# Two-layer trunk in split fp32r on one core: another warm-up for TensorE ahead of the first product

## The chip, the cores and the metric

The kernel runs on one core of a Trainium2 chip. The metric is the device time of one execution in microseconds (us). Three executions of the kernel before are shown; their median is 2297.53 us.

## The reference, cut to what matters

One sequence of 256 tokens of width 2048 passes through two layers. Layer 0 mixes tokens with a gated MLP (a causal 128 x 128 matrix for each of 16 groups of channels), layer 1 with dilated attention (24 heads of 128, three dilations). Behind each stands a gated FFN with a causal convolution of width 3. The matrix products are nearly all of the work:

```
h = x
h = h + gmlp(rms_norm(h))          # w_in 2048 x 4096, w_s 16 x 128 x 128, w_out 2048 x 2048
h = h + conv_ffn(rms_norm(h))      # w_gate, w_up 2048 x 5632, w_down 5632 x 2048
h = h + dilated_attention(rms_norm(h))   # w_qkv 2048 x 9216, w_o 1024 x 2048
h = h + conv_ffn(rms_norm(h))
return rms_norm(h)
```

Everything is float32.

## The kernel before

Activations lie transposed, with channels on the 128 partitions and the 256 tokens along the row. Each float32 operand is split in two fp32r parts, a high one (a rounded copy) and a low one (the rest). `X[:, kt, :]` holds 512 columns: 256 of the high part, then 256 of the low part.

All weights come as one stream of 784 units of 512 KB. A unit is eight tiles of 128 x 128 side by side. SP loads unit after unit into a ring of four slots (`raw`); ACT rounds a unit into `w_hi` (line 439), DVE subtracts and writes `w_lo` (line 728), and PE then works through the eight tiles in `multiply` (lines 1017 to 1028). Two matmuls belong to each tile: line 1026 multiplies `w_hi` with all 512 columns, line 1027 multiplies `w_lo` with the 256 high columns and adds into the same bank. ACT may write a slot of `w_hi` only when PE has finished the unit before in that slot (`units_done`), and SP loads a slot again when `w_lo` has been made from it (`lo_ready`).

The order is fixed by the program text of each engine; there is no planner. PE goes through V and U of the gated MLP (256 pairs of matmuls each), its output product (256), gate and up of the first FFN (1408), down (704), eight heads of attention (144 each), the output product (128), and the second FFN (1408 + 704), 6272 pairs in all. Into this stream the small matmuls of the norms (`mean_square`, plain float32, lines 1048 to 1053), the token mixing, the transposes and the attention scores are set at written places. Long stretches are loops (`Fori`).

At the start ACT issues five loads of `x`, makes the high part of `X` (line 565), and squares `h` for the first norm, with the splits of units 2 to 5 set between the squares. DVE zeroes `hidden`, `warm_r` and `warm_b`, then makes the low part of `X` (`x_low`, line 744) and the `w_lo` of the units. POOL clears small tiles, adds the squares up, and then loads `WS` and `BS`. The tiles `warm_r` and `warm_b` lie where `GX` is written much later. PE waits for both to be zeroed and runs its warm-up (lines 1080 to 1082) into bank `acc[1][:, 1]`, which the first product needs only in its second pair of output blocks and then starts afresh: 16 matmuls of 512 columns and 8 of 128 in fp32r, and 6 of 512 in bf16. Then it waits for `cleared` and `ident_set`, and starts the V product, whose every tile waits for its block of `X` (`x_ready`).

Of the kernel before, what the change touches and what calls it, by code (L numbers as in the profile page):

```python
# [31 lines left out]
F32R = mybir.dt.float32r  # L32
BF16 = mybir.dt.bfloat16
# [4 lines left out]
P = 128  # L38
S = 256
D = 2048  # L40
KT = D // P
# [87 lines left out]
def trunk(nc, w_stream, x_t, vecs_d, ws_t, bs_row, mask_d, rope_d, out):  # L129
    with ExitStack() as ctx:  # L130
# [3 lines left out]
        def sem(name):  # L134
            return ctx.enter_context(nc.semaphore(name))
# [35 lines left out]
        def place(name, at, shape, dt=F32):  # L171
            assert at + int(np.prod(shape[1:])) * 4 <= arena_bytes
            return nc.alloc_sbuf_tensor_at(name, shape, dt, offset=arena_at + at)
# [3 lines left out]
        BLK = S * 4  # L177
# [3 lines left out]
        at = 4 * KT * BLK  # L181
# [5 lines left out]
        vsum = place("vsum", at + 4 * BLK, [P, 2, S])  # L187
        ln_rinv = place("ln_rinv", at + 6 * BLK, [P, S])

        warm_r = place("warm_r", 2 * KT * BLK, [P, 2 * S], F32R)  # L190
        warm_b = place("warm_b", 2 * KT * BLK + 2 * BLK, [P, 2 * S], BF16)

        OX = place("OX", 0, [P, HEADS, 2 * S], F32R)
        at = HEADS * 2 * BLK
# [20 lines left out]
        acc = [ctx.enter_context(nc.psum_tensor(f"acc{i}", [P, 2, 2 * S], F32)) for i in range(2)]  # L215
# [29 lines left out]
        warm_set = sem("warm_set")  # L245
# [185 lines left out]
        def _(act):  # L431
# [218 lines left out]
            def softmax_exp(h_):  # L650
                for t, (a, b, _) in enumerate(score_parts):
                    act.wait_ge(maxed, 2 * h_ + t + 1)
                    nc.scalar.activation(sm[:, a:b], sm[:, a:b], ACT.Exp, bias=nmax[:, t:t + 1],
                                         accum_out=rsum[:, t:t + 1]).then_inc(exped, 1)
# [66 lines left out]
        def _(dve):  # L721
# [102 lines left out]

            nc.vector.memset(warm_r[:, :].bitcast(F32), 0.0).then_inc(warm_set, 1)
            nc.vector.memset(warm_b[:, :], 0.0).then_inc(warm_set, 1)

            dve.wait_ge(vecs_landed, 16)
            x_low(0, 0)
# [111 lines left out]
            def mask_scores(h_):  # L941

                dve.wait_ge(mask_landed, 16)
                dve.wait_ge(scored, h_ + 1)
                for a, b, c in score_parts:
                    nc.vector.scalar_tensor_tensor(sm[:, a:b], sc_flat[:, c:c + b - a], float(E) ** -0.5, mask[:, a:b],
                                                   ALU.mult, ALU.add).then_inc(masked, 1)
                for t, (a, b, _) in enumerate(score_parts):
                    dve.wait_ge(masked, 2 * h_ + t + 1)
                    nc.vector.reduce_max(nmax[:, t:t + 1], sm[:, a:b], AX_X, negate=True).then_inc(maxed, 1)  # L950

            def normalize(h_):

                dve.wait_ge(exped, 2 * h_ + 2)
                nc.vector.reciprocal(rrec[:, :], rsum[:, :]).then_inc(rsum_inv, 1)
                dve.wait_ge(rsum_inv, h_ + 1)
                for t, (a, b, _) in enumerate(score_parts):
                    nc.vector.tensor_scalar(sm[:, a:b], sm[:, a:b], rrec[:, t:t + 1], None, ALU.mult)\
                        .then_inc(normed, 1)
# [56 lines left out]
        def _(pe):  # L1016
# [60 lines left out]
                                    pe.wait_ge(hid_ready, FB * (layer + 1) + 1)  # L1077
                            multiply(ud + 44 * i + 11 * c + n, (11 * c + n) % RING, tiles_of(c % 2, hid, FB, n), needs)

            pe.wait_ge(warm_set, 2)  # L1080
            for n, (tile, cols) in enumerate(((warm_r, 512),) * 16 + ((warm_r, P),) * 8 + ((warm_b, 512),) * 6):
                nc.tensor.matmul(acc[1][:, 1, 0:cols], tile[:, 0:P], tile[:, 0:cols], start=True, stop=True)
            pe.wait_ge(cleared, 5)
            pe.wait_ge(ident_set, 1)
            product(U_V, P_V, KT // 2, X, KT, normed_ready(0), 0, ms_at=5)
# [257 lines left out]
```

## Time and profile before

| | before |
|---|---|
| three executions | 2297.53, 2315.18, 2285.84 us |
| the profiled execution: its span | 2297.4 us |
| its own time beside that span | the median of the runs shown is 2297.53 us |
| mean granted TensorE clock | 0.997 |
| PE busy | 2277.3 us (99%) |
| DVE, ACT, POOL busy | 1488.4, 1272.9, 104.4 us |
| 784 weight loads | 413 MB with the rest of queue q1, 54.0% of 16 DMA engines |

PE is TensorE's matmul stream, PEld its weight loads, which overlap it. Matmul ends are modelled, so one matmul's duration is longer than the distance to the next one's start; distances between starts are the safer measure. PEclk is the clock granted to TensorE, where 1.00 is 2.4 GHz and 0.50 is 1.2 GHz. In a window, a count in brackets takes in an instruction that began before the window and ended in it.

### The profile page before, as it was taken

The page shows a single profiled execution, that of the slowest core. Times are in us where ns is not written, and L with a number is a line of the kernel's source. Part 1 is how long each engine was busy: PE and PEld are TensorE (multiplying, and loading weights), DVE is VectorE, ACT ScalarE, POOL GpSimd, SP SyncE. Part 2 cuts the span into 40 slices and gives each one's busy share as a digit, 9 for nine tenths or more (in the row PEclk, how much of TensorE's full clock was granted, in tenths as well). Part 3 has the DMA queues.
Part 4 walks back from the last instruction along what each step waited for, and adds up shares of the span by engine and source line. Part 5 has one row for each costly group of instructions (what it writes and reads, how often), then busy time and mean ns, then how long its engine had stood idle before and what let it go on. Part 6 is the DMA issues. An engine that isn't in the chain of part 4 may idle for free.

```text
span 2297.4 us, 38095 instructions
## 1 busy us (share of the span) xinstructions
PE 2277.3 (99%) x13098; PEld 1990.5 (87%) x13098; DVE 1488.4 (65%) x1764; ACT 1272.9 (55%) x1587; POOL 104.4 (5%) x85
## 2 busy tenths in 40 slices
PE   8999999999999999999999999999999999999998
PEld 6888888888888888888888888888888888888887
DVE  6678666666666655556666666687677666665444
ACT  5455466666666644444555545556666666654443
POOL 3122100000000000000000000010000000000000
PEclk8999999999999999999999999999999999999999
DMA  6544555555555555555545545546555555556553
GB/s 242 192 161 163 189 184 183 183 188 186 185 188 184 184 190 184 185 178 209 166 166 170 167 165 172 169 153 195 189 191 184 191 191 191 187 189 192 188 188 136
DMA packets 115477, 419.21 MB, mean 182 GB/s; under 512 B 12832, under 2 KB 12960, under 8 KB 115168
## 3 DMA queue, kind: packets, MB, share of 16 engines
q1 hardware_dynamic: 114192, 413.43, 54.0%
q0 software_dynamic: 512, 2.95, 0.3%
q10 hardware_dynamic: 720, 2.10, 0.2%
q8 instruction: 37, 0.61, 0.1%
q14 instruction: 16, 0.13, 0.0%
HBM read 416.33 MB, written 2.10 MB: 182 GB/s over the span
## 4 chain that ended last, share of the span: by engine, by line
PE 96%; DVE 1%; POOL 1%; issue 1%; ACT 0%; DMA 0%; ACTq 0%; DVEq 0%; POOLq 0%
PE acc L1026 61%; PE acc L1027 31%; DVE X L744 1%; POOL vsum L402 1%; PE sc_ps L1164 0%; PE sc_ps L1144 0%; PE sc_ps L1151 0%; DMA h<-x_t 0%; PE acc L1207 0%; PE sc_ps L1159 0%; PE sc_ps L1143 0%; PE misc L1135 0%; DMA raw<-w_stream 0%; DVE w_lo L728 0%; ACT U L600 0%
## 5 line engine op out<-in xcount | busy, mean ns | idle before, releaser
L1026 PE MATMUL acc<-X,w_hi 128*128 128x512 f32 x4480 | 1582.8, 398 | 7.6 <-DVE X L744 6.4
L728 DVE TENSOR_TENSOR w_lo<-raw,w_hi 128x1024 fp32r<-128x1024 f32 x784 | 969.4, 1242 | 527.1 <-ACT w_hi L439 526.3
L1027 PE MATMUL acc<-X,w_lo 128*128 128x256 f32 x4480 | 1256.6, 281 | 0.0
L439 ACT ACTIVATE w_hi<-raw 128x1024 fp32r<-128x1024 f32 x784 | 825.4, 1058 | 469.7 <-PE acc L1027 462.7
L1026 PEld LDWEIGHTS acc<-X,w_hi 128*128 128x128 f32 x4480 | 842.1, 188 | 208.2 <-DVE X L744 5.6
L1027 PEld LDWEIGHTS acc<-X,w_lo 128*128 128x128 f32 x4480 | 848.5, 189 | 0.4
L1026 PE MATMUL acc<-hid,w_hi 128*128 128x512 f32 x1408 | 492.9, 395 | 0.0
L1027 PE MATMUL acc<-hid,w_lo 128*128 128x256 f32 x1408 | 394.9, 281 | 0.0
L1026 PEld LDWEIGHTS acc<-hid,w_hi 128*128 128x128 f32 x1408 | 264.0, 187 | 61.8
L1027 PEld LDWEIGHTS acc<-hid,w_lo 128*128 128x128 f32 x1408 | 266.4, 189 | 0.0
L449 ACT ACTIVATE hc<-acc 128x512 f32<-128x512 f32 x104 | 62.1, 597 | 160.0 <-PE acc L1027 160.0
L733 DVE TENSOR_TENSOR tsum<-hc,acc 128x512 f32<-128x512 f32 x104 | 71.5, 687 | 101.3 <-ACT hc L449 101.3
L367 POOL TENSOR_TENSOR ssum<-ssum,sq 128x512 f32<-128x512 f32 x24 | 33.1, 1378 | 1293.3 <-ACT sq L452 1293.3
L1026 PE MATMUL acc<-GX,w_hi 128*128 128x512 f32 x256 | 90.6, 399 | 1.0 <-DVE GX L863 1.0
L509 ACT ACTIVATE conv<-gu,vecs 128x256 f32<-128x256 f32 x88 | 53.0, 603 | 62.8 <-DVE gu L752 62.8
L752 DVE TENSOR_TENSOR gu<-tsum,rinv 128x512 f32<-128x512 f32 x104 | 72.4, 696 | 3.6
L1027 PE MATMUL acc<-GX,w_lo 128*128 128x256 f32 x256 | 71.9, 281 | 0.0
L632 ACT ACTIVATE hc<-acc 128x512 f32<-128x512 f32 (+1 forms) x40 | 22.2, 555 | 82.1 <-PE acc L1027 82.1
L459 ACT ACTIVATE X<-h,vecs x48 | 21.8, 502 | 73.8 <-DVE h L761 73.5
L1026 PEld LDWEIGHTS acc<-GX,w_hi 128*128 128x128 f32 x256 | 48.1, 188 | 13.1 <-DVE GX L863 1.3
L744 DVE SCALAR_TENSOR_TENSOR X<-h,vecs,X (+1 forms) x64 | 43.5, 707 | 23.1 <-ACT X L459 19.6
L439 ACT ACT_TABLE_LOAD x44 | 56.5, 1283 | 0.9
(141 smaller groups left out, 1080.2 us busy)
## 6 DMA issues: line engine op xcount, KB each, us to landing
raw<-w_stream SPq DMA_DIRECT2D x784, 512.0 KB, 3.4
out<-out_sb SPq DMA_DIRECT2D x8, 256.0 KB, 2.8
h<-x_t ACTq DMA_DIRECT2D x3, 512.0 KB, 6.9
WS<-ws_t POOLq DMA_DIRECT2D x1, 1024.0 KB, 8.1
BS<-bs_row POOLq DMA_DIRECT2D x1, 1024.0 KB, 11.1
mask<-mask_d POOLq DMA_DIRECT2D x1, 576.0 KB, 3.8
h<-x_t ACTq DMA_DIRECT2D x2, 256.0 KB, 4.7
rope<-rope_d POOLq DMA_DIRECT2D x1, 256.0 KB, 3.0
```

The costliest lines, as they stand in the source:

```text
L367: nc.gpsimd.tensor_tensor(ssum[:, :], ssum[:, :], sq[:, :, :].rearrange("p a b -> p (a b)"), ALU.add).then_inc(ss_added, 1)
L402: nc.gpsimd.tensor_tensor(vsum[:, :, :], vsum[:, :, :], U[:, 12 + 2 * k:14 + 2 * k, :], ALU.add)\
L439: nc.scalar.activation(w_hi[slot][:, :], raw[slot][:, :], ACT.Copy).then_inc(hi_ready, 1)
L449: nc.scalar.activation(hc[:, :, :], acc[s][:, :, 0:S], ACT.Copy).then_inc(hcopied, 1)
L509: nc.scalar.activation(conv[:, :], gu[:, 0, 2:S + 2], ACT.Identity, bias=vecs[:, one(cv + 3 * FB + j)], scale=vecs[:, one(cv + 2 * FB + j) ...
L632: nc.scalar.activation(hc[:, 0:n, :], acc[(par + m) % 2][:, 0:n, 0:S], ACT.Copy).then_inc(hcopied, 1)
L728: nc.vector.tensor_tensor(w_lo[slot][:, :], raw[slot][:, :], w_hi[slot][:, :], ALU.subtract)\
L733: nc.vector.tensor_tensor(tsum[:, :, :], hc[:, :, :], acc[s][:, :, S:2 * S], ALU.add)\
L744: nc.vector.scalar_tensor_tensor(X[:, 2 * pr + b, S:2 * S], h[:, 2 * pr + b, :], vecs[:, one(GAINS[n] + 2 * pr + b)], X[:, 2 * pr + b, 0:S ...
L752: nc.vector.tensor_tensor(gu[:, :, 2:S + 2], tsum[:, :, :], over(rinv, 2), ALU.mult)\
L1026: nc.tensor.matmul(bank, hi, moving[:, kt, :], start=first, stop=False)
L1027: op = nc.tensor.matmul(bank[:, S:2 * S], lo, moving[:, kt, 0:S], start=False, stop=last)
```

## The change

The warm-up is replaced by a longer one on larger zero tiles. `warm_r` grows from 512 to 4096 columns, a plain float32 tile `warm_n` of 512 columns is added, and PE waits for three memsets in place of two. The eight 128-column matmuls go. Behind the other 22 come: the pattern of a tile in `multiply` (512 columns, then 256 added into the upper half of the bank), eight times for each of eight shifts of the moving operand (0 to 128 columns) and eight times each for two passes that read it backwards; 16 matmuls of 512, 12 of 256 and 8 of 384 columns; four times two of 512 and two of 256; four of 512 and four of 256 in plain float32; and eight of 512 whose moving operand is two halves 512 columns apart. All write the same bank of `acc[1]`. Nothing that the output depends on is changed.

```
@@ trunk: tiles
-        warm_r = place("warm_r", 2 * KT * BLK, [P, 2 * S], F32R)
-        warm_b = place("warm_b", 2 * KT * BLK + 2 * BLK, [P, 2 * S], BF16)
+        warm_r = place("warm_r", 2 * KT * BLK, [P, 8 * 2 * S], F32R)
+        warm_n = place("warm_n", 2 * KT * BLK + 16 * BLK, [P, 2 * S])
+        warm_b = place("warm_b", 2 * KT * BLK + 18 * BLK, [P, 2 * S], BF16)
@@ vector
             nc.vector.memset(warm_b[:, :], 0.0).then_inc(warm_set, 1)
+            nc.vector.memset(warm_n[:, :], 0.0).then_inc(warm_set, 1)
@@ tensor
-            pe.wait_ge(warm_set, 2)
-            for n, (tile, cols) in enumerate(((warm_r, 512),) * 16 + ((warm_r, P),) * 8 + ((warm_b, 512),) * 6):
+            pe.wait_ge(warm_set, 3)
+            for n, (tile, cols) in enumerate(((warm_r, 512),) * 16 + ((warm_b, 512),) * 6):
                 nc.tensor.matmul(acc[1][:, 1, 0:cols], tile[:, 0:P], tile[:, 0:cols], start=True, stop=True)
+
+            bank = acc[1][:, 1, :]
+            M0 = 2048
+
+            def w_tile(n):
+                return warm_r[:, n % 8 * P:(n % 8 + 1) * P]
+
+            def pairs(shift, count=8, back=False):
+                for n in range(count):
+                    at = M0 + shift + n % 2 * 512
+                    first, second = warm_r[:, at:at + 512], warm_r[:, at:at + S]
+                    if back:
+                        first, second = warm_r[:, at + 511:at - 1:-1], warm_r[:, at + S - 1:at - 1:-1]
+                    nc.tensor.matmul(bank, w_tile(2 * n), first, start=True, stop=False)
+                    nc.tensor.matmul(bank[:, S:2 * S], w_tile(2 * n + 1), second, start=False, stop=True)
+
+            def single(cols, count, at=M0):
+                for n in range(count):
+                    nc.tensor.matmul(bank[:, 0:cols], w_tile(n), warm_r[:, at:at + cols], start=True, stop=True)
+
+            for shift in (0, 2, 4, 8, 16, 32, 64, 128):
+                pairs(shift)
+            pairs(0, back=True)
+            pairs(4, back=True)
+            single(512, 8)
+            single(512, 8, M0 + 4)
+            single(256, 12)
+            single(384, 8)
+            for n in range(4):
+                for k in range(2):
+                    nc.tensor.matmul(bank, w_tile(4 * n + k), warm_r[:, M0:M0 + 512], start=True, stop=True)
+                for k in range(2):
+                    nc.tensor.matmul(bank[:, 0:S], w_tile(4 * n + 2 + k), warm_r[:, M0:M0 + S], start=True, stop=True)
+            for cols in (512, 256):
+                for n in range(4):
+                    nc.tensor.matmul(bank[:, 0:cols], warm_n[:, n * P:(n + 1) * P], warm_n[:, 0:cols], start=True, stop=True)
+            for n in range(8):
+                view = warm_r[:, M0:M0 + 1024].rearrange("p (a b) -> p a b", b=512)[:, :, 0:S]
+                nc.tensor.matmul(bank, w_tile(n), view, start=True, stop=True)
```

## Rows read from the trace of the kernel before

**Rows 1.** The profile's page: header, busy time by engine and the chain of waits by engine.
```profile
span 2297.4 us, 38095 instructions
PE 2277.3 (99%) x13098; PEld 1990.5 (87%) x13098; DVE 1488.4 (65%) x1764; ACT 1272.9 (55%) x1587; POOL 104.4 (5%) x85
PE 96%; DVE 1%; POOL 1%; issue 1%; ACT 0%; DMA 0%; ACTq 0%; DVEq 0%; POOLq 0%
```

**Rows 2.** Timeline of DVE from 0: start us, us, engine line op out<-in xcount [idle before].
```profile
1.27 0.48 DVE L825 MEMSET warm_r<- 128x512 f32 x1
1.76 0.27 DVE L826 MEMSET warm_b<- 128x256 uint32 x1
5.41 0.88 DVE L744 SCALAR_TENSOR_TENSOR X<-h,vecs,X 128x256 fp32r<-128x256 f32 x2 [3.38 <-ACT X L565]
```

**Rows 3.** Timeline of PE, then a window: length, PE busy (count), PEclk.
```profile
2.08 6.10 PE L1082 MATMUL acc<-warm_r 128*128 128x512 f32 x24 [2.08 <-DVE warm_b L826]
8.03 1.47 PE L1082 MATMUL acc<-warm_b 128*128 128x512 bf16 x6
9.40 0.47 PE L1026 MATMUL acc<-X,w_hi 128*128 128x512 f32 x1
...
2.10:5.10 3.00, 3.00 (x7) 1.00 0.86 285
```

**Rows 4.** Windows of PE through the start.
```profile
20.00:26.00 6.00, 3.56 (x9) 0.50 0.00 0
28.00:30.00 2.00, 2.00 (x11) 0.80 0.56 201
```

**Rows 5.** Timeline of PE, then of DVE, 15 to 30 us.
```profile
15.92 0.76 PE L1026 MATMUL acc<-X,w_hi 128*128 128x512 f32 x1 [3.50 <-DVE X L744]
29.09 0.40 PE L1026 MATMUL acc<-X,w_hi 128*128 128x512 f32 x1
...
15.29 8.37 DVE L744 SCALAR_TENSOR_TENSOR X<-h,vecs,X 128x256 fp32r<-128x256 f32 x8
```

**Rows 6.** Timeline of PE around 34 us and the first mean square.
```profile
34.02 0.40 PE L1026 MATMUL acc<-X,w_hi 128*128 128x512 f32 x1
34.27 0.28 PE L1027 MATMUL acc<-X,w_lo 128*128 128x256 f32 x1
34.39 0.40 PE L1026 MATMUL acc<-X,w_hi 128*128 128x512 f32 x1
...
38.63 1.03 PE L1052 MATMUL misc<-ssum,mean_w 128*128 128x256 f32 x4
39.84 0.40 PE L1026 MATMUL acc<-X,w_hi 128*128 128x512 f32 x1
```

**Rows 7.** Windows of line 1026 alone: length, PE busy (count), PEld busy (count), PEclk.
```profile
29.09:38.62 9.53, 9.53 (x28) 4.96 (x27) 1.00 0.87 323
40.00:142.00 102.00, 101.37 (x293) 54.75 (x292) 1.00 0.57 191
320.00:1097.00 777.00, 776.38 (x2198) 412.77 (x2198) 1.00 0.56 186
1123.00:1153.00 30.00, 30.00 (x86) 15.96 (x85) 1.00 0.50 172
1515.00:1555.00 40.00, 40.00 (x114) 21.24 (x113) 1.00 0.56 184
1566.00:2285.00 719.00, 719.00 (x2076) 387.88 (x2075) 1.00 0.56 185
```

**Rows 8.** Timeline of ACT, DVE and POOL around 30 us.
```profile
30.41 1.06 ACT L439 ACTIVATE w_hi<-raw 128x1024 fp32r<-128x1024 f32 x1 [4.00 <-PE acc L1027]
...
34.32 1.23 DVE L728 TENSOR_TENSOR w_lo<-raw,w_hi 128x1024 fp32r<-128x1024 f32 x1 [1.59 <-ACT w_hi L439]
...
29.19 0.70 POOL L379 DMA_DIRECT2D WS<-ws_t  x1
```

**Rows 9.** Timeline of PE at 145 us.
```profile
145.16 1.13 PE L1100 MATMUL misc<-vsum,mean_w 128*128 128x256 f32 x4 [2.02 <-POOL vsum L402]
```

## The prediction, made before the result was known

> **What bounds the kernel now.** First the header, the engine totals and the chain of waits [rows 1]: the span is 2297.4 us, PE is busy for 99% of it, and 96% of the chain that ended last is PE. So time changes here in two ways only: PE is handed more or less work, or one piece of work takes PE longer. The profiled execution took the 2297.53 us that is also the median of the three runs shown (2285.84 to 2315.18), so the sum is made against 2297.5.
>
> Second, the start. The zero tiles are set by 2.03 us [rows 2], PE's old warm-up runs from 2.08 to 9.4 us and the first real product starts at 9.40 [rows 3]. But PE is not fed yet: it stands still for 3.50 us before 15.92, its granted clock falls from 1.00 to 0.50 (2.4 to 1.2 GHz), at half clock it is busy for 3.56 of 6.00 us between 20 and 26, and it is back at full clock within the window from 28 to 30 [rows 4, 5]. From 29.09 us on nothing holds it. The products (called pairs here: a 512-column matmul with `w_hi` and a 256-column one with `w_lo`) that started before 29.09 number 21 (eight of unit 0, eight of unit 1, five of unit 2). At the 0.35 us of a pair [rows 6] these are 7.4 us of work. So the start up to 29.09 is worth as much as a PE that begins fully fed at 29.09 - 7.4 = **21.7 us**. That is the number against which a longer warm-up is priced: up to there it costs nothing, since PE would be waiting anyway.
>
> Third, the long stretches at line 1026, where each row counts hi matmuls in a window [rows 7]. They show two rates at the same full clock and with PE busy throughout: 777 us for 2198 from 320 us on (353.7 ns a pair, the one that began before the window left off; first FFN), 719 us for 2076 from 1566 on (346.5 ns; second FFN). Both stages run the same code on operands of the same shapes. Short stretches are of one kind or the other: 9.53 us for 27 before the first mean square is slow (353), 102 us for 293 behind it quick, 40 us for 114 slow again (354). The rate does not drift; it changes where the stream of pairs is broken by a wait or by other matmuls, and then stays. I call this the **spacing**, and it is the only thing in this trace that could make the three runs differ by 29 us: one FFN layer has 2112 pairs, and 2112 x 6.6 to 7.2 ns is 14 to 15 us. The shown profile has one layer slow and one quick.
>
> **The change part by part.**
>
> *Memsets.* DVE sets `warm_r` with 4096 elements a partition in place of 512, and `warm_n` with 512. 512 took 0.48 us and the 256 words of `warm_b` took 0.27 [rows 2], so 0.82 ns for each further element: 0.48 + 3584 x 0.82 ns = 3.4 us, and 0.48 for `warm_n`. The DVE queue is then at 1.27 + 3.4 + 0.27 + 0.48 = 5.4 us. Behind them in that queue stands the first `x_low`, which started at 5.41 after 3.38 us of waiting for ACT: hidden, with no margin. PE waits for all three and starts at 5.45 rather than 2.08.
>
> *PE's new warm-up.* Removed: eight 128-column matmuls. Kept: 16 of 512 in fp32r, six in bf16. Added: 80 pairs (eight shifts and two reversed passes, eight each), 16 + 8 (mixed) + 8 (strided view) of 512, 12 + 8 of 256, 8 of 384, and in plain fp32 four of 512 and four of 256. Prices at full clock: a hi matmul takes its successor 0.23 us later and a lo one 0.12 us later, 0.35 together [rows 6]; 384 columns lie between, 0.175; the six bf16 took 1.37 us [rows 3]; the mean square, two plain fp32 matmuls of 256, put the next pair but one from 38.63 to 39.84, 1.21 us where a pair takes 0.35, so 0.43 us for 256 plain columns and 0.86 for 512 [rows 6].
> 80 x 0.35 = 28.0; 48 of 512 x 0.23 = 11.0; 20 of 256 x 0.12 = 2.4; 8 x 0.175 = 1.4; bf16 1.4; plain 4 x 0.86 + 4 x 0.43 = 5.2. Sum **49.4 us**.
> The first stretch runs at half clock: in the first 3.00 us of the old warm-up only seven fell, 0.43 us each [rows 3], twice the 0.23 of later rows. If the new one needs the same 3 us to be given the full clock, that is seven matmuls by 0.2: 1.4 us more. Warm-up ends at 5.45 + 49.4 + 1.4 = **56.2 us**.
>
> A rule bears on this term. The Trainium skill (TensorE: Matmul & The Clock Gate, Back-to-back issue gap) gives N / 2.4 + 2.5 ns for a warm matmul; as an estimate from that page the non-plain 97,280 columns would take 41.1 us where my rows give 44.2, and the end would be near 53 us. The rows for fp32r with its weight load each time decide here.
>
> *Unknown forms.* No row of the trace shows a shifted, reversed or strided fp32r read. Lower end: they cost as a plain one, since the array takes one column after another. Upper end: the nearest row for a slow read of four-byte data is plain fp32, 0.43 us per 256; a pair would be 1.3 us. For the 16 reversed pairs alone that is 16 x 0.95 = + 15 us; for the 56 shifted ones too, and the eight views at 0.86, + 74. I take the lower end: the row nearest in type and size is the fp32r pair itself. By the Trainium skill (SBUF — State Buffer, on the 16-byte lines) reads that hit a line at least twice run at full bandwidth; a reversed or shifted run of fp32 hits most lines four times, which also speaks for it.
>
> *What starts when PE is free.* Everything that held PE up to 28.8 us is done while it warms: `x_low` ends at 23.66 [rows 5], and the two `w_lo` splits behind it, 1.23 us each [rows 8], fill the last of the four slots before 27. Unit 4's slot comes free only when unit 0 is done. That is 8 x 0.35 = 2.8 us after the warm-up; ACT 1.06 and DVE 1.23 [rows 8] make it ready 5.1 us after, and it is wanted after 32 pairs, 11.2 us. In ACT's queue the squares of blocks 12 to 15 stand behind that split, so POOL's last two sums and its issue of the `WS` and `BS` loads behind them, at 29.19 before, slip to some 7 us after the warm-up (2.8, then 1.06 for the split, then the squares and sums); before they stood 29.2 - 21.7 = 7.5 us after the equivalent start [rows 8]. So they keep their place against PE, and the mean square, GELU sums and the 2.02 us wait at 145.16 [rows 9] move along unchanged. SP's queue gets its loads earlier than it needs. No stall is added and none but those of the start goes.
>
> *Sum.* 56.2 - 21.7 = + 34.5 us, so 2297.5 + 34.5 = **2332 us** (+ 1.5%), if each later stretch keeps the spacing it has.
>
> **The rivals.**
>
> 1. *Base case, 2332* (2322 to 2340 from the clock and the price of 128 to 512 columns). For it: the start is a clean sum. Whatever the warm-up does to the spacing is overwritten early: the first two windows [rows 7] show that the mean square at 38.63 alone changes it, and more breaks follow, as the wait at 145 [rows 9]. Chance 0.44.
>
> 2. *Slow side, over + 2%: the second FFN draws the slow spacing.* Place: the break at about 1558 us where the normed activations are waited for. Price: 2112 x 6.6 to 7.2 ns = 14 to 15 us, so 2332 + 14.5 = 2346. In the windows the stretch just ahead of that break is slow and the one behind it quick [rows 7], so the break is what set it. It decides as soon as that one layer is slow and the first one has not turned quick. The highest of the three runs, 17.7 us over the median, looks like this case. A like sum comes if the reversed pairs cost as plain fp32 does: 2347. Chance 0.26 together.
>
> 3. *The warm-up works: PE is left in the quick spacing and keeps it.* Then the slow stretches shown (2198 + 114 counted pairs, and 86 in each of eight heads [rows 7], together 3000) lose some 7 ns each: - 21 us, 2311. With the first FFN alone quick, 2317. The lowest run, 11.7 us under the median, looks like this half. Against it: breaks follow the warm-up and each of the heads repeats its own changes of spacing whatever came before. Still + 0.5% or more, since 34.5 is more than all there is to win. Chance 0.25.
>
> 4. *Faster than before.* It needs a spacing that no row shows: from 346 ns down to 320 (768 columns at 2.4 GHz) the 6272 pairs would lose 163 us, 2169. It decides from 6 ns a pair on average. Nothing in the trace speaks for it. Chance 0.03.
>
> 5. *The change does not do what it says*: the warm-up ends inside the 21.7 us in which PE has nothing to do, and the time stays at 2298. It would need less than half of the price of every row above. Chance 0.02.
>
> **How the numbers follow.** What a measurement of this kernel can tell is about 2%, 46 us: slower means above 2343.5. That is rival 2: 0.26. Faster, below 2251.6, is rival 4: 0.03. The rest, 0.71, is within. The predicted time is the base case. The range goes down to rival 3 with the short stretches that I left out (2310) and up to just past rival 2 (2349).
>
> **What would show it.** In the new profile: PE's first matmul at about 5.4 us; the first real product at 56 us (54 to 60); granted clock 1.00 from about 8 us on without a fall; no PE idle from there to the mean; the shifted and reversed groups with the mean of the unshifted ones; then two or three long windows whose length over count is either 346 to 348 or 352 to 354 ns. The span minus (old span + delay of the first real matmul against 21.7) must equal the pairs that changed spacing times 6.6 to 7.2 ns. I am wrong if the first real matmul comes after 65 us (forms cost), or if the spacing takes a new value.

## The result and the profile after

| | before | changed |
|---|---|---|
| executions | 2285.84, 2297.53, 2315.18 us | 2321.56, 2335.11, 2350.81 us |
| median | 2297.53 us | 2335.11 us |
| span of the profiled execution | 2297.4 us | 2319.8 us |
| PE busy | 2277.3 us (99%) | 2300.9 us (99%) |

The changed kernel takes 1.0146 times the time of before, 95% interval 1.0074 to 1.0218: slower, by 1.5% as measured, with 2% still inside the interval. The forecast was 2332 us in a range of 2310 to 2349; the median lies 3 us above the one and inside the other, the slowest execution 2 us outside. One execution of a later kernel, at a mean granted clock of 0.851 (2467.67 us, its other eleven at most 2301.32), is left out of every figure below. The profiled execution is the fastest of the three (2321.56 us), so its rows must be read beside one execution of the kernel before that was in the middle of its three.

The page after, header, engine totals and chain by engine, against [rows 1]:

```profile
span 2319.8 us, 38552 instructions
PE 2300.9 (99%) x13326; PEld 2018.3 (87%) x13326; DVE 1490.8 (64%) x1765; ACT 1270.0 (55%) x1587; POOL 103.9 (4%) x85
PE 97%; DVE 1%; POOL 1%; ACT 0%; issue 0%; DVEq 0%; ACTq 0%; POOLq 0%
```

PE still sets the end alone. Its queue starts later, behind three memsets. DVE's timeline after, against [rows 2]:

```profile
2.02 3.47 DVE L826 MEMSET warm_r<- 128x4096 f32 x1 [0.80 <-issue]
5.49 0.27 DVE L827 MEMSET warm_b<- 128x256 uint32 x1
5.82 0.48 DVE L828 MEMSET warm_n<- 128x512 f32 x1
6.22 0.75 DVE L745 SCALAR_TENSOR_TENSOR X<-h,vecs,X 128x256 fp32r<-128x256 f32 x2
```

The long memset took 3.47 us (3.4 forecast), but it began at 2.02 and not at 1.27. `x_low` slipped from 5.41 to 6.22. PE's timeline and two windows of line 1098 (the hi matmuls of the 80 pairs; length, PE busy with the count, PEld busy with the count, PEclk, DMA share, GB/s), against [rows 3]:

```profile
6.36 5.30 PE L1084 MATMUL acc<-warm_r 128*128 128x512 f32 x16 [6.36 <-DVE warm_n L828]
11.51 1.47 PE L1084 MATMUL acc<-warm_b 128*128 128x512 bf16 x6
```

```profile
12.62:35.00 22.38, 22.38 (x64) 12.01 (x64) 1.00 0.36 123
35.00:40.60 5.60, 5.60 (x17) 2.95 (x16) 1.00 0.00 0
```

```profile
57.24 0.40 PE L1028 MATMUL acc<-X,w_hi 128*128 128x512 f32 x1
```

The old part of the warm-up starts at 6.36. The window from 12.62 to 35.00 holds the eight shifts: 22.38 us for 64 pairs, 0.350 us each. The one from 35.00 to 40.60 holds the starts of the two reversed passes (16 hi matmuls; the seventeenth began before). It ends within a pair, so their price is better read from start to start:

```profile
34.93 0.40 PE L1098 MATMUL acc<-warm_r 128*128 128x512 f32 x1
...
40.94 0.62 PE L1103 MATMUL acc<-warm_r 128*128 128x512 f32 x2
```

From the last shifted pair to the first matmul behind the reversed ones lie 17 pairs in 6.01 us, 0.354 each. The groups of eight shifted pairs lie between 0.346 and 0.354. The first real product starts at 57.24. Windows of PE alone (length, busy with the count, PEclk), against [rows 4]:

```profile
6.40:9.40 3.00, 3.00 (x7) 1.00 1.02 419
14.00:57.00 43.00, 43.00 (x230) 1.00 0.16 58
57.00:80.00 23.00, 23.00 (x133) 1.00 0.49 187
1576.00:1578.50 2.50, 0.38 (x3) 1.00 0.56 184
1579.40:1582.80 3.40, 3.40 (x13) 0.51 0.64 219
```

In the first window the seven 512-column matmuls are 0.43 us apart, twice the 0.23 of later ones, as in [rows 3]: they ran at half clock although the column says 1.00. From 14 to 80 us PE is busy without a gap and the clock does not fall. It falls once, much later: PE had little to do from 1576.0 to 1578.5, and the 3.4 us behind 1579.4 ran at a granted clock of 0.51, close to the 1.2 GHz level. Last, line 1028 alone, which is line 1026 of before, against [rows 7]:

```profile
76.00:142.00 66.00, 66.00 (x191) 35.64 (x191) 1.00 0.56 193
258.00:353.00 95.00, 95.00 (x270) 50.51 (x270) 1.00 0.56 187
356.00:1117.00 761.00, 760.37 (x2194) 411.15 (x2193) 1.00 0.56 190
1588.00:2308.00 720.00, 720.00 (x2078) 388.37 (x2078) 1.00 0.55 185
```

Less the one that began before, 95 us for 269 is 353 ns a pair, 761 for 2193 is 347, 720 for 2077 is 346.7. In this execution **both** feed-forward layers have the quick spacing; in the one shown of before only the second had.

### The profile page after: what moved, and what is told of

It is laid out like the page before. It is cut to its first block, busy times and chain, and to the rows that moved or that the text cites. A ratio compares the mean times of both kernels' runs of the same rounds, so it can differ in the third digit from the quotient of the medians.

```text
span 2319.8 us, 38552 instructions
## 1 busy us (share of the span) xinstructions
PE 2300.9 (99%) x13326; PEld 2018.3 (87%) x13326; DVE 1490.8 (64%) x1765; ACT 1270.0 (55%) x1587; POOL 103.9 (4%) x85
## 4 chain that ended last, share of the span: by engine, by line
PE 97%; DVE 1%; POOL 1%; ACT 0%; issue 0%; DVEq 0%; ACTq 0%; POOLq 0%
PE acc L1028 61%; PE acc L1029 31%; PE acc L1098 1%; POOL vsum L403 1%; PE sc_ps L1205 0%; PE sc_ps L1185 0%; PE acc L1099 0%; PE sc_ps L1192 0%; PE acc L1084 0%; PE acc L1103 0%; PE acc L1248 0%; PE sc_ps L1200 0%; PE sc_ps L1184 0%; PE misc L1176 0%; PE acc L1120 0%
```

## The experiments

Twelve runs followed, one of them the changed kernel again. The kernel before ran beside them and, with its first three, has 97 executions. They fall on three levels with nothing between:

| level | range, us | mean | executions of before |
|---|---|---|---|
| low | 2281.67 to 2289.33 | 2285.0 | 41 |
| middle | 2297.53 to 2303.31 | 2300.5 | 35 |
| high | 2312.35 to 2317.30 | 2315.0 | 21 |

The steps are 15.5 and 14.5 us; the prediction had 14 to 15 us for one feed-forward layer at the other spacing. The traces bear that out. In all 14 of them a layer's loop runs at 346.7 or at 353.3 ns a pair from start to start. Nine executions with no slow layer are at the low level of their kernel, three with one (the first) at the middle one, and two with both at the high one. Theory 1 was: the delay is the warm-up's length past 21.7 us, and the level is drawn later, at breaks of PE's stream. Theory 2: the warm-up, or its forms, sets the spacing.

### No warm-up

```
-            for n, (tile, cols) in enumerate(((warm_r, 512),) * 16 + ((warm_r, P),) * 8 + ((warm_b, 512),) * 6):
-                nc.tensor.matmul(acc[1][:, 1, 0:cols], tile[:, 0:P], tile[:, 0:cols], start=True, stop=True)
```

> The kernel before without any warm-up matmul (the output is not touched by them). Theory 1 (time is the length of the warm-up past the start that the data allow, and spacing is redrawn at later waits whatever the warm-up was): PE begins the first eight pairs at half clock, which ends inside its own wait; the pairs from 29.09 us on stand as before, so the time is that of the kernel before within 2 us at the same spacing, on one of its three levels (2285, 2298, 2313). Theory 2 (the warm-up sets the spacing of the later stages): without it both feed-forward layers take one and the same spacing in every execution, most likely the slow one, 2311 to 2316 each time.

Ten executions: one at 2284.39, seven from 2299.97 to 2302.21, two at 2314.43 and 2314.78. Against before 1.0022 (0.9974 to 1.0071). Windows of PE, columns as above, and the longest wait of PE up to 40 us (total, times, longest):

```profile
9.20:13.40 4.20, 4.11 (x13) 1.00 0.96 344
16.00:24.00 8.00, 4.76 (x15) 0.75 0.21 72
24.00:29.00 5.00, 3.80 (x12) 0.50 0.28 105
29.00:33.00 4.00, 4.00 (x21) 0.84 0.81 248
```

```profile
PE acc L1026 <- DVE w_lo L728: 10.5, 2, 9.3
```

Full clock comes about 1.5 us later than before (within 29 to 33 at 0.84, where before the window from 28 to 30 had 0.80), and the first mean square starts at 39.07, where before it was 38.63 [rows 6]. So the old warm-up bought 0.4 us, next to nothing, as the reckoning with 21.7 us says, and all three levels appear without it.

The row from 9.2 to 13.4 reads 1.00, but the first pairs ran at half clock, as expected:

```profile
10.07 0.63 PE L1026 MATMUL acc<-X,w_hi 128*128 128x512 f32 x1
10.71 0.63 PE L1026 MATMUL acc<-X,w_hi 128*128 128x512 f32 x1
...
13.26 0.39 PE L1026 MATMUL acc<-X,w_hi 128*128 128x512 f32 x1
```

Their starts are 0.64 us apart up to 12.63 and 0.35 behind 13.26. Ahead of the first change of clock in a trace the distances must be read, not the column PEclk. Theory 2 falls in its plain form.

### As long, of one form

```
-            for shift in (0, 2, 4, 8, 16, 32, 64, 128):
-                pairs(shift)
...
-                nc.tensor.matmul(bank, w_tile(n), view, start=True, stop=True)
+            pairs(0, 127)
```

> The changed kernel with its many forms replaced by as long a stretch of one form: 22 old matmuls, then 127 unshifted pairs. Theory 1: the forms are nothing, the length all; first real product at 57 us (56.5 to 58), time on the same three levels as the changed kernel (2321, 2335, 2350), and breaks later redraw the spacing. Theory 2: the later spacing goes by the forms, so all executions come out alike and off those of the changed kernel, at the slow level, 2350.

```profile
57.67 0.40 PE L1028 MATMUL acc<-X,w_hi 128*128 128x512 f32 x1
```

First real product at 57.67 us; four executions at 2320.75, 2321.89, 2333.28 and 2335.65; 1.014 of before (1.0039 to 1.024). The same delay and the low and middle levels of the changed kernel. The unshifted pairs are 0.353 us apart here, start to start, so the reversed ones above (0.354) cost no more. The forms can be exchanged without a trace in the time; four executions are too few to say anything of the shares.

### Cut to what the start hides

```
-        warm_r = place("warm_r", 2 * KT * BLK, [P, 8 * 2 * S], F32R)
+        warm_r = place("warm_r", 2 * KT * BLK, [P, 4 * 2 * S], F32R)
...
+            pairs(0)
+            pairs(4)
+            pairs(0, back=True)
```

(in place of all groups behind the first 22 matmuls, with `M0 = 512`)

> The changed warm-up cut to what the start hides: 22 old matmuls, then 8 unshifted, 8 shifted by 4 and 8 reversed pairs, on a warm_r of 2048 columns. It should end near 20 us. Theory 1: the granted clock does not fall in the first 30 us, the pairs of unit 1 and 2 run at 0.35 instead of 0.64, and the first product that nothing holds comes at most 1 us sooner against its count; time on the levels of the kernel before, less 0 to 1 us. The rival to the sum: the warm-up costs its own length wherever it ends, so + 11 us (19.5 less the old end of 9.4), levels 2296, 2309, 2324.

```profile
10.00:20.00 10.00, 10.00 (x56) 1.00 0.76 261
20.00:26.00 6.00, 5.93 (x35) 1.00 0.01 3
26.00:30.00 4.00, 3.61 (x20) 1.00 0.50 153
```

The first real product starts at 20.22 us, 10.8 us later than before, and the time does not follow: executions from 2281.22 to 2286.41 (five), 2297.27 to 2299.86 (four), 2312.28; 0.9974 of before (0.9921 to 1.0027). The rival sum, + 11 us, is out. The clock stays at 1.00 through 30 us and PE has 35 matmuls between 20 and 26 where it had 9 [rows 4]. The first pair behind the first 21 starts at 28.26 us by the trace, where before it was 29.09 [rows 5]: 0.8 us won. The levels lie some 1 to 3 us lower; the interval does not settle that.

### Twice the pairs

```
-            def pairs(shift, count=8, back=False):
+            def pairs(shift, count=16, back=False):
```

> The changed kernel with 16 pairs in place of 8 in each of the ten groups of pairs, 80 pairs more. Theory 1: + 80 x 0.35 = 28 us on the first real product (85 us) and on the end, levels 2349, 2363, 2378, with shifted and reversed pairs at the same 0.35 as unshifted ones. Rival: part of the delay is given back later because the weights are ahead and the queues are full, then less than + 20 us; or the longer dose of forms settles the spacing, then all executions at the lowest level, 2349.

```profile
86.28 0.40 PE L1028 MATMUL acc<-X,w_hi 128*128 128x512 f32 x1
```

First real product at 86.28: 29.0 us behind that of the changed kernel for 80 pairs. Of this 0.9 us lies in the 22 old matmuls, whose slow first stretch was longer here (the first pair starts at 13.52 and not at 12.62); the rest is 0.352 a pair, shifted and reversed ones among them. Executions 2347.28, 2365.33, 2376.90, 2377.10; median 2371.12; 1.030 (1.0181 to 1.0418). Past the hidden part the price is one to one within 3 us: before's mean levels plus 64.6 us (86.28 less 21.7) would be 2349.6, 2365.1 and 2379.6. Nothing like 8 us is given back, and a double dose of the forms does not keep the kernel at its lowest level.

### Four small breaks in each feed-forward layer

The kernels from here on, but for the changed kernel's second run, put a few matmuls on dummy data into PE's stream of pairs. Two of them have the short warm-up as well, the others that of before:

```
+            def settle_spacing():
+                for _ in range(2):
+                    nc.tensor.matmul(sc_ps[:, 2, 0:P], mean_w[:, :], mean_w[:, :], start=True, stop=True)
+                for _ in range(2):
+                    nc.tensor.transpose(sc_ps[:, 1, 0:P], mean_w[:, :], ident[:, :])
+            def after_unit(n, k, ms_at):
+                if k == ms_at:
+                    mean_square(n)
+                if n in (1, 3) and k in BREAKS:
+                    settle_spacing()
...
-            two_pairs(u0, p0, moving, k_tiles, needs, (lambda k: mean_square(n) if k == ms_at else None)
+            two_pairs(u0, p0, moving, k_tiles, needs, (lambda k: after_unit(n, k, ms_at))
```

with `BREAKS = (4, 5, 6, 7)`.

> The kernel before with its old warm-up. In each feed-forward layer, behind units 4, 5, 6 and 7 of gate and up, PE gets the small matmuls of one step of the U stage on dummy data: two plain fp32 of 128 columns and two 128-column transposes into a bank that nothing reads. In the U stage these came 13 times in a row with quick spacing on both sides, and once turned slow into quick. Cost by those rows: 0.67 us each, 5.3 us for eight. Theory 1 (spacing is a phase of PE's own stream, set at breaks, kept in loops): both layers quick in every execution, one level near 2285 + 5 = 2290 in place of three, median some 8 us under the kernel before. Rival (spacing comes from outside PE, from the state of the weight stream or the memory): three levels as before, each 5 us higher, 2290, 2306, 2321.

Twelve executions: eleven from 2289.50 to 2293, one at 2306.05; median 2291.84 and 0.9995 of before (0.9958 to 1.0032). Eleven of twelve are at one level, as theory 1 has it; "every execution" and the median 8 us under before are misses. The 35 executions of before beside them were low in 22 cases (5 middle, 8 high) with a median of 2285.30, so this median lies 6.5 us above it, and by the ratio the breaks cost what they save.

### One break in each layer

`BREAKS = (4,)`.

> The same with one such break in each layer, behind unit 4. Theory 1: one break maps slow to quick only in part of the phases; mostly the low level, 2286, with some executions at 2301, cost 1.3 us. Rival: three levels as before, each 1.3 us higher.

```profile
324.00:1082.00 758.00, 757.37 (x2185) 408.41 (x2184) 1.00 0.58 191
1556.00:2271.00 715.00, 715.00 (x2064) 385.74 (x2063) 1.00 0.57 186
```

(Windows of its hi line in the two layers.) 758 us for 2184 pairs is 347 ns, 715 for 2063 is 346.6: both quick. Executions: ten from 2285.24 to 2287, two at 2302; median 2286.11, 0.9981 (0.9942 to 1.0020). The matmuls cost a quarter. Ten of twelve are low beside 22 of 35 of before, which alone settles little; over this kernel, the last and the next together, it is 32 of 36, and none is high.

### The short warm-up with four breaks

> The short warm-up that the start hides (22 old matmuls and 24 pairs) together with the four breaks in each layer. Both parts add up if they are independent: one level, 2283 + 5 = 2288 (2286 to 2291), the lowest median of all kernels so far. If the breaks do nothing: 2288, 2304, 2317.

Eleven executions from 2286.18 to 2293, one at 2305.01; median 2289.36, 0.9988 (0.995 to 1.0026). The median lies where the sum of both parts had the level (2286 to 2291). "The lowest median so far" is a miss: one break without the short warm-up had 2286.11.

### Four breaks in the second layer alone

```
-                if n in (1, 3) and k in BREAKS:
+                if n == 3 and k in BREAKS:
```

> The kernel before with the four breaks in the second feed-forward layer alone. Theory 1: that layer always quick, the first as it falls: two levels, 2285 + 2.7 = 2288 and 2303, none at 2318. Rival: three levels.

Nine from 2286.39 to 2289, two at 2303, one at 2319.69; median 2287.23, 0.9987 (0.9938 to 1.0035). "None at 2318" is a miss by one in twelve: the breaks do not always hold. The profiled execution has both layers quick. This one settles little, since the first layer fell quick in most executions anyway.

### The changed kernel again

> The changed kernel once more, for more executions. Theory 1 (the forms do nothing to the later spacing): three levels near 2321, 2335 and 2350, with shares as mixed as those of the kernel before beside it. Rival (the forms help to the quick spacing): nearly all executions at 2321.

```profile
360.00:1130.00 770.00, 769.37 (x2178) 409.05 (x2177) 1.00 0.56 187
1605.00:2337.00 732.00, 732.00 (x2073) 389.27 (x2072) 1.00 0.55 182
```

Six executions, four from 2334.99 to 2337.11 and two at 2351; median 2337.04, 1.0175 (1.0123 to 1.0228). The profiled one (2351.18) has 770 us for 2177 pairs (353.7) and 732 for 2072 (353.3): both layers slow, on the same instructions with which both were quick above. So the long warm-up does not fix the level. Over the 17 executions with a long warm-up (changed, one form, twice) the levels are 4 low, 8 middle, 5 high, against 41, 35, 21 for before. That it makes the low level rarer can't be read from so few.

### The short warm-up with one break

> The candidate that should beat both: the short warm-up that the start hides and one break of small matmuls (two plain fp32 of 128 columns, two transposes) behind unit 4 in each feed-forward layer. Low level 2283 + 1.3 = 2284 to 2285 in at least 10 of 12 executions, some at 2299, none above. If the two parts are not independent: shares like those of the kernel before.

Nine executions from 2282.98 to 2287.76 and two at 2301; at least ten low ones were expected. Median 2286.49 with before at 2300.52 beside it: 0.9958 (0.9923 to 0.9993), the first ratio whose interval lies below 1. How much is won hangs on what before draws, though: here it was low in 6 of 23 executions, beside the three kernels with one or four breaks in both layers in 22 of 35, and there nothing was won.

### A break of two kinds, meant to slow it

```
-            def settle_spacing():
+            def settle_spacing(turns=2):
...
-                for _ in range(2):
+                for _ in range(turns):
                     nc.tensor.transpose(sc_ps[:, 1, 0:P], mean_w[:, :], ident[:, :])
...
+                if n in (1, 3) and k == 5:
+                    settle_spacing(0)
```

> The kernel before with the same break behind unit 4 and, behind unit 5, the two plain fp32 matmuls alone, in each feed-forward layer. In the U stage the matmuls without the transposes turned quick spacing into slow in the traces of before and of the changed kernel. Theory 1 (the kind of break and the phase ahead of it decide): both layers slow in nearly every execution, 2285 + 29 + 1.3 + 0.9 = 2316, though it is only 0.9 us of matmuls more than the kernel with one break. Rival (breaks redraw at random): three levels, 2287, 2302, 2316, with mixed shares.

```profile
330.00:1085.00 755.00, 754.37 (x2176) 407.84 (x2176) 1.00 0.57 191
1562.00:2274.00 712.00, 712.00 (x2055) 385.12 (x2054) 1.00 0.56 186
```

The expectation fell, with theory 1's forecast as I had put it and the rival both. All twelve executions lie between 2285.66 and 2289.95: 755 us for 2175 pairs is 347, 712 for 2054 is 346.6, both quick. Median 2288.82 with before at 2300.52 beside it, 0.9956 (0.9929 to 0.9984), the other kernel whose interval lies below 1, by the same luck of before's draw, and the only one with a single level at the quick side. What failed was the rule from the U stage. There the same two matmuls stand alone twice, and counted over all 14 traces the first of the two turned quick into slow in 11 of 11 cases; in this trace too, while in its feed-forward layers they left quick as it was:

```profile
213.92 0.61 PE L1124 MATMUL sc_ps<-WS,vt 128*128 128x128 f32 x4
214.28 0.48 PE L1027 MATMUL acc<-X,w_hi 128*128 128x512 f32 x1
...
214.71 0.39 PE L1027 MATMUL acc<-X,w_hi 128*128 128x512 f32 x1
...
216.83 0.40 PE L1027 MATMUL acc<-X,w_hi 128*128 128x512 f32 x1
...
327.70 0.61 PE L1052 MATMUL sc_ps<-mean_w 128*128 128x128 f32 x4
328.06 0.47 PE L1027 MATMUL acc<-X,w_hi 128*128 128x512 f32 x1
```

Both times a full break and eight quick pairs stand ahead, the shapes and the bank are the same, and the two matmuls take 0.36 us. Behind 213.92 the six steps from 214.71 to 216.83 are 353 ns each, behind 327.70 the layer runs at 346.7. What differs are the operands (`WS`, `vt` against `mean_w` on both sides), the columns of the bank that the second product writes, and whatever finer state the stream is in. So neither the kind of the matmuls nor the length of the break decides alone.

### A break of two kinds, with the transposes alone

```
-            def settle_spacing():
+            def settle_spacing(products=2):
...
-                for _ in range(2):
+                for _ in range(products):
                     nc.tensor.matmul(sc_ps[:, 2, 0:P], mean_w[:, :], mean_w[:, :], start=True, stop=True)
...
+                if n in (1, 3) and k == 5:
+                    settle_spacing(0)
```

> As the last one, but behind unit 5 the two transposes alone, without the matmuls. Counted over all thirteen traces so far: the full break in the feed-forward layers led to quick spacing in 26 of 26 cases, and two transposes alone, in the U stage, turned the quick spacing behind such a break into slow in 9 of 11. Theory 1 (the sequence of matmuls in a break decides, whatever the data and the wait before): both layers slow in most executions, level 2285 + 29 + 1.3 + 0.5 = 2316, some at 2302. Rival (two breaks in a row always settle the spacing at quick, as the pair with the matmuls did): one level at 2287.

```profile
322.79 0.61 PE L1052 MATMUL sc_ps<-mean_w 128*128 128x128 f32 x4
323.24 0.38 PE L1054 MATMUL sc_ps<-ident,mean_w 128*128 128x128 f32 x2
323.38 0.48 PE L1027 MATMUL acc<-X,w_hi 128*128 128x512 f32 x1
...
326.24 0.38 PE L1054 MATMUL sc_ps<-ident,mean_w 128*128 128x128 f32 x2
326.38 0.48 PE L1027 MATMUL acc<-X,w_hi 128*128 128x512 f32 x1
```

(Timeline of PE in the first feed-forward layer: the full break at 322.79, the transposes alone at 326.24.)

```profile
330.00:1097.00 767.00, 766.37 (x2170) 407.42 (x2169) 1.00 0.56 187
1575.00:2300.00 725.00, 725.00 (x2053) 385.56 (x2052) 1.00 0.54 183
```

767 us for 2169 pairs is 353.6, 725 for 2052 is 353.3: both layers slow. All twelve executions lie between 2313.48 and 2317.39, median 2315.65; 1.0063 of before (1.0034 to 1.0091). Beside the kernel with one break this one has four more transposes of 128 columns in all, which add some 0.5 us (at 326.24 the two take 0.14 from start to next start and the pair behind them is 0.08 longer), and takes 29.5 us more (2315.65 against 2286.11; the kernel before stood on the same three levels beside both). Beside the last kernel the only difference is two transposes in place of two matmuls behind unit 5: twelve of twelve executions at the high level against twelve of twelve at the low one. So what PE itself is given in a short break sets the spacing for the next 2000 pairs, some 700 us, in a layer with a wait of PE ahead of it (the second) and in one without (the first). That it does so whatever the data is not shown; the two places in the trace of the kernel before this one speak against it. The rival, one level at 2287, is out. One reading of the expectation above needs a correction: in the U stage no full break stands ahead of the lone transposes. Counted over the thirteen traces of that time, they met quick spacing 15 times there and left it slow 12 times.

## Why the prediction was right

**The bound and the equivalent start held.** The time follows the first real product only past 21.7 us: at 20.22 us it costs nothing, at 57.24 and 86.28 it costs 1 for 1.

**The sum held, with one small term off; that the median fell beside it is in part luck.** The warm-up itself took 57.24 - 6.36 = 50.9 us; 49.4 + 1.4 = 50.8 were forecast. The memset term missed 0.9 us, since DVE began the long memset at 2.02 and not 1.27. So the delay was 35.5 us, not 34.5. As an estimate, the Trainium skill (TensorE: Matmul & The Clock Gate, Back-to-back issue gap), by its formula for the isolated gap of a warm matmul, would have put it 3 us shorter; the rows of fp32r matmuls that each load their own weights decided rightly. The level is drawn anew in each execution: 17 executions with a long warm-up fell 4, 8 and 5 times on the three levels, so a median of three could as well have come out near 2321 or 2351. The forecast named the middle level as its base case with 0.44; that this one came is luck, the delay of 35 us on every level is not.

**The unknown forms cost as plain ones:** 0.350 us a pair shifted and 0.354 reversed, against 0.353 unshifted in the kernel with one form, all on zeros. The Trainium skill (SBUF — State Buffer, Specifications (TRN2), on the 16-byte lines) asks for at least two accesses to a 16-byte line for full bandwidth. A contiguous run of fp32 makes four on most lines; the trace agrees for these shifts and for both directions.

**From delay to end.** In the two profiled executions the span grew by 22.4 us, and landmarks take that apart. The first feed-forward layer's mean square starts at 318.39 before and at 353.47 after: 35.1 us later. The next norm's, behind the layer's 2112 pairs, starts at 1065.50 and 1086.50: 21.0 later, since 14.1 (2112 pairs by 6.7 ns) were won. The second layer's first product starts at 1557.65 and 1578.51, 20.9 later; its mean square, 18 pairs on, at 1564.05 and 1586.48, 22.4 later. So the stretch at half clock cost 1.6 us, and behind it nothing changes any more. The prediction's sign, "granted clock 1.00 from about 8 us on without a fall", missed this one.

The profiled execution is thus the half of the forecast's rival 3 in which the first feed-forward layer alone turns quick, by its rows; the median of the three is the base case and the slowest, 2350.81, is rival 2, both by their levels. The text had 2317, 2332 and 2346, and 2321.6, 2335.1 and 2350.8 came. The 3 to 5 us between them are the 1.0 us of the later start and the base: 2297.5 was one execution, while the mean of the middle level is 2300.5. Before's mean levels plus 35.5 are 2320.5, 2336.0 and 2350.5.

**Where the working was weaker than its result.** The prediction said that a break redraws the spacing, and stopped there. Counted over all 14 traces, breaks are not alike.

The mean square of the feed-forward layers met quick spacing 14 times and left it quick 14 times; it met slow spacing 14 times and left it slow 7 times. The full break met quick spacing 175 times, in the U stage and in the layers, and always left it quick. Of 49 meetings with slow spacing it ended 7: two of two in the layers, five of 47 in the U stage, where three traces stayed slow through all 14 such breaks. In the layers the spacing ahead of the breaks was thus already quick in 26 of 28 cases, and the two cases that turned are few; that the breaks turn slow into quick there rests mostly on the levels (53 of 59 executions low in the five kernels with breaks in both layers that came out quick).

What differs between slow phases, why 6 of those 59 still missed one layer, and what in the hardware makes a pair of matmuls last 353 or 347 ns, stays open. Shown is that a change of two instructions in a break moves both layers from one spacing to the other.

**Rival 3's mechanism** (the warm-up leaves PE quick and it stays so) is refuted: same instructions, one execution with both layers quick and one with both slow.

**Rival 4's bound was mis-sized.** "It decides from 6 ns a pair" is where the kernel would equal before (34.5 us by 6272 pairs is 5.5 ns). To fall below 2251.6 from 2332 it takes 80.4 us, 12.8 ns a pair. Nothing hung on it.

## What to carry to other kernels

Price a warm-up against the time at which the first engine could run unhindered, not against the old start: up to there it is free, and behind it each microsecond is one. When executions of one kernel fall on separate levels, count matmuls per long window at full clock before looking for a cause outside: a 2% difference in spacing over a loop is such a level. A few small matmuls where a long uniform stream begins can fix the level, for less than a microsecond each, but which ones must be tried in their place, since a neighbour of the good sequence fixed the bad level. Whether that pays depends on how often the kernel is slow without them. Compare levels and not medians alone: the kernel before had its median at 2285.30 beside one set of runs and at 2300.52 beside another.

## What the runs showed of the hardware that was not expected

- A stream of alternating 512- and 256-column fp32r matmuls, each with its own weight load, runs at 346.7 or 353.3 ns a pair at the same granted clock of 1.00 and keeps its rate for over 2000 pairs.
- Whether two transposes or two plain fp32 matmuls of 128 columns stood at one place of each layer made 27 us in kernels that are otherwise alike (2315.65 against 2288.82).
- The granted clock fell to 0.51 for 3.4 us behind a wait of PE of only 2.13 us (ending at 1578.51 in the changed kernel). The wait at that place was 2.11 to 2.13 us in six traces, and in five of them the clock fell. In the sixth it did not, and neither did it in the eight whose wait was 1.26 to 1.40 us. The changed kernel's two runs, the same program (timelines of PE, then a window of the second run with its granted clock; the first run's window from 1579.40 stands in the section on the result):

```profile
1578.51 0.50 PE L1028 MATMUL acc<-X,w_hi 128*128 128x512 f32 x1 [2.13 <-DVE X L745]
1595.74 0.50 PE L1028 MATMUL acc<-X,w_hi 128*128 128x512 f32 x1 [2.13 <-DVE X L745]
1595.74:1600.74 5.00, 5.00 (x28) 1.00 0.77 238
```

- Moving operands of fp32r read backwards, or from a start shifted by 2 to 128 columns, cost nothing extra (0.354 and 0.350 us a pair, unshifted 0.353).
